# A mixture-of-experts phase with weights in three 4 MB pieces a block, a ring of three, and one bias product a block

## The reference

```python
logits = hf @ router_w + router_b; top, eidx = top_k(logits, 4); gates = softmax(top)
# the rows are sorted by expert, each expert's rows padded to whole blocks
def expert_block(xb, e):
    gu   = xb @ w_gu[e] + b_gu[e]                     # 1024 -> 2 x 1024
    gate = minimum(gu[:, :1024], 7.0)
    up   = clip(gu[:, 1024:], -7.0, 7.0)
    act  = gate * sigmoid(1.702 * gate) * (up + 1)
    return act @ w_down[e] + b_down[e]                # 1024 -> 1024
y = x + sum over the 4 choices of gates * expert row
```

## Time and profile before

| | us |
|---|---|
| three runs | 1972.93, 1968.89, 1969.58 |
| median | 1969.58 |
| profiled execution, its own time | 1974.51 |
| span in that execution | 1972.5 |
| mean granted TensorE clock | 0.949 of full |
| busy: PE, PEld, DVE, ACT, POOL | 1822.6, 1031.1, 525.9, 350.3, 375.9 |
| transfers over the whole span | 541.77 MB |

### The profile page before, as it was taken

How to read it: one execution, slowest core, us unless ns; L and a number is a source line. 1 busy time by engine, 2 the same in 40 slices (tenths; PEclk the granted TensorE clock), 3 DMA queues, 4 the chain that set the end, 5 groups by cost and what they waited for, 6 DMA issues and landing times.

```text
span 1972.5 us, 40602 instructions
## 1 busy us (share of the span) xinstructions
PE 1822.6 (92%) x16769; PEld 1031.1 (52%) x16769; DVE 525.9 (27%) x1305; ACT 350.3 (18%) x758; POOL 375.9 (19%) x434
## 2 busy tenths in 40 slices
PE   7998996779799999979999999999999999999990
PEld 3546884454488886543444444444454745454440
DVE  2223325346311111262121221212121212212125
ACT  3232432355400000100110111111111101011110
POOL 0010101147400001401212121212222121212222
PEclk9997998889799999977999999999999999999995
DMA  8206924450241113138999999999999999999937
GB/s 302 92 10 214 402 92 168 174 198 1 84 152 54 54 33 110 66 153 358 410 414 419 414 419 406 418 408 417 413 415 402 414 418 412 414 411 410 414 142 280
DMA packets 74368, 541.77 MB, mean 275 GB/s; under 512 B 17520, under 2 KB 22480, under 8 KB 46897
## 3 DMA queue, kind: packets, MB, share of 16 engines
q1 hardware_dynamic: 61913, 485.54, 61.2%
q0 software_dynamic: 11664, 51.42, 6.6%
q10 hardware_dynamic: 624, 2.23, 0.3%
HBM read 520.49 MB, written 30.62 MB: 279 GB/s over the span
## 4 chain that ended last, share of the span: by engine, by line
PE 52%; DVE 1%; DMA 1%; issue 1%; POOL 0%; POOLq 0%; ACT 0%; SPq 0%; DVEq 0%
PE psum L2720 34%; PE psum L2736 17%; PE psum L2766 1%; DVE arena L2707 1%; DMA arena<-scr_h,arena 0%; DMA arena<-y_of 0%; DVE arena L2713 0%; DMA y_of<-arena 0%; POOL arena L2634 0%; DVE arena L2712 0%; DVE arena L2665 0%; POOL arena L2604 0%; POOLq L2539 0%; ACT arena L2654 0%; SPq L2582 0%
## 5 line engine op out<-in xcount | busy, mean ns | idle before, releaser
L2720 PE MATMUL psum<-arena 128*32 128x512 f32 x6144 | 668.8, 593 | 0.0
L2720 PEld LDWEIGHTS psum<-arena 128*32 128x32 f32 x6144 | 232.3, 109 | 417.2 <-issue 412.5
L2736 PE MATMUL psum<-arena 128*32 128x256 f32 x6144 | 338.4, 378 | 0.0
L2736 PEld LDWEIGHTS psum<-arena 128*32 128x32 f32 x6144 | 242.1, 109 | 103.2 <-issue 17.5
L2682 DVE TENSOR_SCALAR arena<-psum 128x256 f32<-128x256 f32 x96 | 38.3, 399 | 786.1 <-PE psum L2720 786.1
L2621 POOL DMA_INDIRECT y_of<-arena x96 | 97.0, 1011 | 556.6 <-ACT arena L2654 556.6
L2380 PE MATMUL psum<-arena 128*128 128x272 f32 x768 | 182.9, 396 | 1.6 <-PEq L224 1.6
L2380 PEld LDWEIGHTS psum<-arena 128*128 128x128 f32 x768 | 146.9, 191 | 35.3 <-issue 3.2
L2650 ACT ACTIVATE arena<-arena 128x256 f32<-128x256 f32 x96 | 40.1, 418 | 644.0 <-DVE arena L2682 644.0
L746 PE MATMUL psum<-arena 128*128 128x512 f32 (+3 forms) x320 | 112.3, 510 | 0.2 <-DVE arena L618 0.2
L2600 POOL DMA_INDIRECT arena<-scr_h,arena x96 | 98.5, 1026 | 48.9 <-POOL arena L2596 28.1
(11 more groups left out here) (356 smaller groups left out, 1512.8 us busy)
## 6 DMA issues: line engine op xcount, KB each, us to landing
arena<-in_w_gu SPq DMA_DIRECT2D x128, 2048.0 KB, 12.0
arena<-in_w_down SPq DMA_DIRECT2D x64, 2048.0 KB, 12.4
arena<-in_w_gb SPq DMA_DIRECT2D x24, 512.0 KB, 3.6
arena<-y_of SPq DMA_DIRECT2D x8, 1024.0 KB, 15.5
arena<-in_w_tok SPq DMA_DIRECT2D x3, 2048.0 KB, 15.4
arena<-in_x_all SPq DMA_DIRECT2D x8, 512.0 KB, 9.9
arena<-in_cache_mem SPq DMA_DIRECT2D x8, 512.0 KB, 11.5
arena<-in_cache_win SPq DMA_DIRECT2D x8, 512.0 KB, 16.0
```

Source lines behind the costliest of these rows:

```text
L2720: mm = pe.matmul(gu_bank(g)[32 * j:32 * j + 32].rearrange("p (h n) -> p h n", h=2), xgT[:, g, 32 * k:32 * k + 32], gu_w(slot)[:, part, :, ...
L2736: mm = pe.matmul(dn_half(g)[32 * j:32 * j + 32], actT[:, g, 32 * k:32 * k + 32], dn_w(slot)[:, part, 256 * j:256 * j + 256], start=(k == 0 ...
```

## The change

- Pieces of 8192 words a partition (4 MB): three a block, two of `w_gu`, one of `w_down`. The ring has three slots, one block.
- The PE loop has one block (`UNROLL` = 1) and no back-edge hint on either level.
- The bias is one product of four matmuls per block into bank 6, for the next block, between `down` of group 0 and of group 1. ACT copies it to `bias_sb`; DVE adds it to the PSUM result of each group ahead of the clamps. The first `into` opens the accumulation.
- x stays on chip: `scr_x`, its writes and reads are gone.
- SP issues the first block's `w_down` at the head of the expert phase, ahead of the wait for `e_sent`.

```diff
-RING_W = 4096
+RING_W = 8192
-WRING = 36864 // RING_W
-UNROLL = 3
+WRING = 24576 // RING_W
+UNROLL = 1
...
-        ring_at = [oT_at - 120 - KD * NTOK, oT_at - 120 - KD * NTOK + 4096, w_gb_at, tail_base + KD * D,
-                   tail_base + KD * D + 4096, tail_base + 2 * KD * D, tail_base, tail_base + 4096, x_at]
+        ring_at = [hT_at, tail_base + KD * D, tail_base]
...
-                for t in range(early):
-                    sp.dma_start(ring[t], weights(slice(0, 1), t)).then_inc(e_in[t], 16)
+                sp.dma_start(ring[0], weights(slice(0, 1), 0)).then_inc(e_in[0], 16)
...
-                        for t in range(early, PER_BLOCK):
-                            sp.dma_start(ring[t], weights(slice(0, 1), t)).then_inc(e_in[t], 16)
+                        sp.dma_start(ring[1], weights(slice(0, 1), 1)).then_inc(e_in[1], 16)
...
             @block.sync
             def _(sp):
+                sp.dma_start(ring[2], weights(slice(0, 1), 2)).then_inc(e_in[2], 16)
                 blocks = used(sp)
                 sp.wait_ge(e_sent, 1)
...
-                sp.wait_ge(e_y, blocks * G + G)
-                for n in ORDER:
-                    sp.dma_start(x_end(n)[0:ROWS[n]], scr_x[128 * n:128 * n + ROWS[n]]).then_inc(y_x, 16)
...
             def _(act):
                 act.sem_inc(e_yc, G)
-                for n in range(NT):
-                    act.wait_ge(p_be, 2 * n + 2)
-                    act.dma_start(scr_x[128 * n:128 * n + ROWS[n]], x[0:ROWS[n], n]).then_inc(p_x, 16)
+                def bias_in(b):
+
+                    act.wait_ge(e_bb, b + 1)
+                    act.activation(bias_sb, bank(6), ACT.Copy).then_inc(e_bc, 1)
+
+                bias_in(0)
...
                                     act.activation(y_rows[:, g], dn_half(g), ACT.Copy, scale=cur_gate[:, g:g + 1]).then_inc(e_yc, 1)
+                                    if g == 0:
+                                        act.wait_ge(e_c, 2 * G * b + 2 * G)
+                                        bias_in(b + 1)
...
                             with dve.If(b < blocks):
+                                dve.wait_ge(e_bb, b + 1)
+                                to_bias_of(b + 1)
                                 for g in range(G):
                                     dve.wait_ge(e_gu, G * b + G + g + 1)
-                                    dve.tensor_scalar(gate_c[:, g], gu_bank(g)[:, 0:256], LIMIT, None, ALU.min).then_inc(e_c, 1)
-                                    dve.tensor_scalar(up_c[:, g], gu_bank(g)[:, 256:512], LIMIT, -LIMIT, ALU.min, ALU.max).then_inc(e_c, 1)
+                                    if g == 0:
+                                        dve.wait_ge(e_bc, b + 1)
+                                    dve.tensor_tensor(gu_c[:, g], gu_bank(g), bias_sb, ALU.add).then_inc(e_ba, 1)
+                                    dve.wait_ge(e_ba, G * b + g + 1)
+                                    dve.tensor_scalar(gate_c(g), gate_c(g), LIMIT, None, ALU.min).then_inc(e_c, 1)
+                                    dve.tensor_scalar(up_c(g), up_c(g), LIMIT, -LIMIT, ALU.min, ALU.max).then_inc(e_c, 1)
...
-                                       start=False, stop=(k == KD - 1), tile_position=(0, 32 * j))
+                                       start=(k == 0), stop=(k == KD - 1), tile_position=(0, 32 * j))
                     return mm
+
+                def bias_out(b):
+
+                    pe.wait_ge(e_bs, b + 1)
+                    pe.wait_ge(e_bc, b)
+                    for j in range(4):
+                        mm = pe.matmul(bank(6)[32 * j:32 * j + 32].rearrange("p (h n) -> p h n", h=2), bias_of[0:96],
+                                       b_parts[0:96].rearrange("p (h n) -> p h n", h=2)[:, :, 256 * j:256 * j + 256],
+                                       start=True, stop=True, tile_position=(0, 32 * j))
+                    mm.then_inc(e_bb, 1)
...
-                with nc.Fori(0, NBLK // 9, engines=PE_ONLY, hint_back_edge=True) as nine:
+                with pe.Fori(0, NBLK // 9) as nine:
                     with pe.If(9 * nine < blocks):
-                        with nc.Fori(0, 9 // UNROLL, engines=PE_ONLY, hint_back_edge=True) as three:
+                        with pe.Fori(0, 9 // UNROLL) as three:
...
-                                    for g in range(G):
-                                        for j in range(4):
-                                            pe.matmul(gu_bank(g)[32 * j:32 * j + 32].rearrange("p (h n) -> p h n", h=2), bias_of[0:96],
-                                                      b_parts[0:96].rearrange("p (h n) -> p h n", h=2)[:, :, 256 * j:256 * j + 256],
-                                                      start=True, stop=False, tile_position=(0, 32 * j))
...
                                     for g in range(G):
                                         down(b, g, i3, u)
+                                        if g == 0:
+                                            bias_out(b + 1)
```

More of the change, by code:

```diff
@@ L2081, in build_program @@
         scr_h = scratch("scr_h", [NTOK, D])
-        scr_x = scratch("scr_x", [NTOK, D])
         y_of = scratch("y_of", [TOPK, 1024, D])
-        ring_at = [oT_at - 120 - KD * NTOK, oT_at - 120 - KD * NTOK + 4096, w_gb_at, tail_base + KD * D,
-                   tail_base + KD * D + 4096, tail_base + 2 * KD * D, tail_base, tail_base + 4096, x_at]
-        ring = [arena[:, at + o:at + o + RING_W] for at in ring_at[:WRING * RING_W // 4096] for o in range(0, 4096, RING_W)]
+        hT_at = oT_at - 120 - KD * NTOK
+        ring_at = [hT_at, tail_base + KD * D, tail_base]
+        end_at = [hT_at, hT_at + 4096, w_gb_at, tail_base + KD * D, tail_base + KD * D + 4096]
+        ring = [arena[:, at:at + RING_W] for at in ring_at]
         e_in = [lasting(f"e_in{n}") for n in range(WRING)]
@@ L2487, in build_program @@
         bias_of = take(32, dt=BF16)
-        gate_c = take(GROUPS_E, 256)
-        up_c = take(GROUPS_E, 256)
+        gu_c = take(GROUPS_E, 512)
+        gate_c = lambda g: gu_c[:, g, 0:256]
+        up_c = lambda g: gu_c[:, g, 256:512]
+        bias_sb = take(512)
         act_h = take(GROUPS_E, 256)
@@ L2500, in build_program @@
         e_bs = sem("e_bs")
+        e_bb, e_bc, e_ba = sem("e_bb"), sem("e_bc"), sem("e_ba")
         e_use = sem("e_use")
@@ L2529, in build_program @@
         dn_w = lambda slot: ring[slot].rearrange("p (k n) -> p k n", k=DN_K)
-        four = lambda n: arena[:, ring_at[n]:ring_at[n] + 4096].rearrange("p (k n) -> p k n", k=TOPK)
-        x_end = lambda n: arena[:, ring_at[5 + n // 4] + D * (n % 4):ring_at[5 + n // 4] + D * (n % 4) + D]
+        four = lambda n: arena[:, end_at[n]:end_at[n] + 4096].rearrange("p (k n) -> p k n", k=TOPK)
+        x_end = lambda n: x[:, n]
         out_p = o["y_prompt"][0]
@@ L2567, in _ @@
                                     sp.wait_ge(e_use, UNROLL * USES * i3 + (USES * (was + 1) + last + 1 - (last >= GU_PARTS)))
-                                if u == 0 and slot * RING_W // 4096 == 8:
-                                    sp.wait_ge(p_x, 16 * NT)
                                 sp.dma_start(ring[slot], weights(bass.ds(e, 1), t)).then_inc(e_in[slot], 16)
@@ L2649, in _ @@
                                     act.wait_ge(e_c, 2 * G * b + 2 * g + 1)
-                                    act.activation(act_h[:, g], gate_c[:, g], ACT.Sigmoid, scale=ALPHA).then_inc(e_sg, 1)
+                                    act.activation(act_h[:, g], gate_c(g), ACT.Sigmoid, scale=ALPHA).then_inc(e_sg, 1)
                                 act.wait_ge(e_ir, 2 * b + 2)
@@ L2665, in to_xgT, with to_bias_of @@
                     dve.transpose(xgT.rearrange("p g n -> p (g n)"), xg.rearrange("p g n -> p (g n)")).then_inc(e_xT, 1)
+                def to_bias_of(b):
                     dve.tensor_copy(bias_of[0:96], e_match[0:96, bass.ds(b, 1)].to_broadcast([96, 32])).then_inc(e_bs, 1)
+                to_bias_of(0)
                 for u in range(2 * NT):
@@ L2748, in _ @@
                               b_down[0:32, 512 * (u % 2):512 * (u % 2) + 512], start=True, stop=True).then_inc(p_bd, 1)
+                pe.wait_ge(e_bs, 1)
+                pe.wait_ge(p_be, 2 * NT)
+                for j in range(4):
+                    mm = pe.matmul(bank(6)[32 * j:32 * j + 32].rearrange("p (h n) -> p h n", h=2), bias_of[0:96],
+                                   b_parts[0:96].rearrange("p (h n) -> p h n", h=2)[:, :, 256 * j:256 * j + 256],
+                                   start=True, stop=True, tile_position=(0, 32 * j))
+                mm.then_inc(e_bb, 1)
                 pe.sem_inc(e_use, USES)
```

13 lines of the change are left out of this document (2 added, 11 removed).

## The result

The changed kernel takes **1943.01 us** (median of 4 runs, 1941.41 to 1945.8) beside 1969.59 us for the kernel before in the same sessions (4 runs, 1968.89 to 1972.93): a ratio of 0.9863, 95% interval 0.9846 to 0.988, so 26.6 us less. The forecast was 1950 in a range of 1943 to 1985: the sign came out, but the gain is larger than the sum by some 7 us. The time lies on the lowest edge of the range: 0.9863 of the 1969.58 us that the forecast started from is 1942.6 us, just outside it.

What follows compares the result with a forecast made beforehand. PE was taken to bound the kernel: -13.8 - 9.35 + 3.1 + 2 - 1.1 = -19.2 us against the profiled 1974.51 gives 1955.3. The median lies 4.9 us lower, so 1950 us, range 1943 to 1985.

Steps and rivals of the forecast that it cites:

- the tail: End of the kernel: without the reload of x the last scatter lands sooner, -1.1 us, bounds 0 to -2.9.
- the bias: PE, each block: four matmuls instead of twelve, 0.43 us less a block, first block's ahead of the loop; -13.8 us together.
- What bounds the kernel: Expert phase: PE sets the pace at 31.62 us a block with no wait for a transfer; the transfers keep up.
- The rival of a DMA bound: Expert phase: transfers stay at 411 GB/s and set 31.6 us a block, +13 us, 1960 in all; chance 0.14.
- Back edges: PE's loop: ten edges of three-block bodies go, -9.35 us; 31 new one-block edges at 0.1 us each add 3.1.
- The rival: PE's loop: each new back edge must refetch its target, 2 us an edge taken, 2009 us in all; chance 0.22.
- Start: Start of the expert phase: 4 MB of weights issued ahead of the first gathers delay the third, +2 us, bounds -1.5 to +5.3.
- The gather chain: Expert phase: gathers and scatters queue behind longer weight packets until PE waits for rows, 1996 us if 1.5 a block; chance 0.07.
- The sign of landings between 12 and 16 us: Expert phase: 4 MB weight pieces landing in 12 to 16 us would show the prediction right.

## Why the prediction was off, and where it was right

The step that failed is the tail: its term, the reload of x at 1.1 us, measured 7.0, of which 4 are shown to come from the reload. The bound on PE, the bias and the old back edges came out as worked out.

**What bounds the kernel** was right. PE's duration per block is the period before, after and with the old bias put back, and the DMA followed at 420 GB/s, above the 416 that the prediction asked of it. The rival of a DMA bound (31.6 us a block) is refuted: the period is 31.19.

**Bias**, -13.8: right. The 0.43 us a block is what the chain shows. The first block took 1.47 + 23.02 = 24.49 us before and takes 23.47 now, so it gave 1.0 us instead of the 0.4 counted; and putting the product back cost 13.8.

**Back edges**, -9.35 and +3.1: the first right, the second too high by 1.4. Inner edges cost 0 and three outer ones 1.7 us. The evidence used (branches inside the loop of three are free, the new body is a third of the old) pointed the right way but did not settle it: as the prediction says, no row showed that the body stays, so that 0.1 was a choice and its near hit is in part luck. The rival fell: the new body of 2.8 packets stays in the engine, and so does one of 5.7. The Trainium skill's two-page rule (Runtime: NRT & Kernel Launch, Instruction fetch mechanics) would have had a fetch at each edge; 36 and 39 packets in the whole program say otherwise, and the measurement decides. The same section's 128 KiB agree: two blocks fit and three don't. And the price that this rival took, 2 us, was far below the 8.5 us measured without the hint for a body of three blocks; if an edge of one block cost as much, its 2009 would have been 1947 + 31 x 8.5 = 2210, an estimate.

**Start**, +2: too high. The third gather took 10.05 us where the earlier trace rows had 9.25, which by itself is the expected direction, but it was issued 0.7 us earlier and the first block's bias now lies in the wait: the first product is at 902.69 where the first bias was at 902.65. The term is 0.

**Tail**, -1.1: this is the step that failed, the largest miss of the sum. It measured -7.0 us (45.4 to 38.4 us). The prediction said of the sums behind the scatter that they are unchanged because "x was already back by then". It was not: the last piece of the reload landed at 1940.2, 6.5 us behind the scatter. What became shorter is both the scatter (5.25 to 2.34, -2.9, the far bound that the prediction named) and the first load of `y_of` behind it (first sum 7.3 and now 3.3 us after the scatter, -4.0, which was in no bound). With the reload back, 4 us returned, all of them in the scatter (6.52 us), and the first sum stayed 3.4 us behind it; the 3 us between that run and the kernel before stay open.

The sum with the measured terms: bias 14.4, edges 9.35 less 1.7 = 7.6, start 0, tail 7.0; 29.0 us, against 28.6 between the spans (the rest is rounding: from the first product to the end of the last the kernel gained 21.7 us). The four terms that missed (bias, new edges, start, tail) did so on the same side, by 0.6, 1.4, 2 and 5.9 us, and nothing cancelled: the profiled execution took 1945.8 us where the sum gave 1955.3. Of these 9.5 us the median shows 7.0, because it lies 2.8 us below the profiled execution and not 4.9. The range was tighter than its own terms: with edges of 0 and the start and the tail at their low bounds the sum gives 1941.6, below the 1943 at which the range begins.

**The gather chain** did not decide, but was nearer than the 0.07 given to it suggests. Its mechanism fits: beside 32 KB packets a scatter takes 8.6 us instead of 6.7, and DVE waits for the gathers in nearly every block, 125 us in all. In the median 2.4 us of slack are left, at the least 1.2, where 2.2 us had been worked out for a gather of the median kind, and in the hinted loop of three one block did wait 1.2 us for a gather. The sign of landings between 12 and 16 us for the `w_gu` pieces came out as far as it can be read: the changed kernel's own profile lists none, but the three runs with the same pieces that do (both with x by way of HBM, and one block with the hint) have medians of 14.9 to 15.2 us.

## What to carry to other kernels

Count a loop body in instruction packets before choosing its length: here bodies of up to two blocks (5.7 packets by the estimate) went round for nothing, one of three blocks (8.5) cost 0.9 to 2.0 us an edge on average with a hint and some 8.5 us without, and a body that fits needs neither unrolling nor hint. Larger weight packets are free only as long as nothing that needs a quick answer (a gather, a scatter) comes late beside them: here they gained nothing, a scatter took 8.6 us beside them instead of 6.7, and little slack was left for the gathers. Undo the parts of a change one at a time, since everything else of this change with the old loop length shows no gain at all (0.9983 of before). When a transfer is taken out of a tail, look up when its last piece landed, not when it was issued: what is issued until then shares the DMA with it.

## What was not expected of the hardware

- An idle of 5.2 us on PE at a back edge was followed by a mean granted clock of 0.88 over the next 23.6 us; of the shorter gaps in the hinted loop of three, one of 2.74 us was followed by a `w_gu` of 20.81 us and one of 1.99 us by one of 22.51 us at a mean clock of 0.92. What decides between these is open.
- The cost of a hinted edge varies with the weight pieces beside it and with the program: ten edges of a 148-packet program cost 20.0 us with 32 KB weight packets, 15.4 with 16 KB ones, and 9.3 with 16 KB ones and the bias products at the head.
- Leaving the inner of two nested loops costs PE 0.55 to 0.67 us although nothing is fetched, 0.82 to 1.09 with hints, and nothing in a loop of one level.
- One core moved 420 GB/s over 938 us, 377.03 of the 393.76 MB on the queue that loads the weights from HBM, with single slices up to 431.
